# A split moved ahead of the last expert product, filler turns ahead of the first, and result rows asked for by SyncE

## The reference, cut to what matters

```python
def grouped_moe(h, router_w, router_b, w1, w3, w2):        # D = 1024, EXPERT_FF = 256
    s = jax.nn.sigmoid(h @ router_w)                       # 16 scores per token
    ...                                                    # best group, two best experts in it, weights that sum to 1
    y = jnp.zeros_like(h)
    for e in range(N_EXPERTS):
        a = jax.nn.silu(h @ w1[e]) * (h @ w3[e])
        y = y + combine[..., e:e + 1] * (a @ w2[e])
    return y

for i in range(DEPTH):                                     # DEPTH = 2
    ...                                                    # h from norm and modulation, four mixers, gates, w_o: x = x + m[:, 2] * mix
    h2 = modulate(rms_norm(x, norm2_g[i]), m[:, 3], m[:, 4])
    x = x + m[:, 5] * grouped_moe(h2, router_w, router_b, moe_w1[i], moe_w3[i], moe_w2[i])
```

## Time and profile before

| | value |
|---|---|
| median of 3 runs | 2329.77 us (2325.93 to 2334.15) |
| the profiled execution's own time | 2335.57 us |
| its span, first to last instruction | 2333.8 us |
| PE busy | 2124.2 us, 91% of the span |
| DVE busy | 1372.8 us, 59% |
| ACT busy | 991.8 us, 42% |
| mean granted TensorE clock | 0.952 of 2.4 GHz |
| expert stage of layer 0 / layer 1 | about 1043 to 1333 us / 2058 to 2305 us of the span |

### The profile page before, as it was taken

One profiled execution on the slowest core, in us unless ns is written; L12 is line 12 of the kernel. 1 busy time (PEld: TensorE's weight loads), 2 busy tenths in 40 slices (PEclk: granted clock), 3 DMA queues, 4 the chain that ended last, 5 costly groups with the idle time before them and its releaser, 6 DMA issues.

```text
span 2333.8 us, 28756 instructions
## 1 busy us (share of the span) xinstructions
PE 2124.2 (91%) x10673; PEld 1719.5 (74%) x10673; DVE 1372.8 (59%) x1496; ACT 991.8 (42%) x1290; POOL 369.5 (16%) x400
## 2 busy tenths in 40 slices
PE   5879999999989999978999766999999999889994
PEld 3646788888778888877878654668888878778783
DVE  2655455666766433367989666453344454469885
ACT  3645411321211122227878655442422223348882
POOL 3300000000000001003555323000000000025552
PEclk7979999999989999988999887999999999999997
DMA  7020044444655232029999452003334344269993
GB/s 278 1 63 1 19 122 136 140 123 132 190 175 150 73 109 90 28 107 369 388 362 383 169 197 72 1 1 81 100 87 108 95 122 131 73 254 368 368 371 132
DMA packets 247398, 360.00 MB, mean 154 GB/s; under 512 B 22528, under 2 KB 180480, under 8 KB 245760
## 3 DMA queue, kind: packets, MB, share of 16 engines
q1 hardware_dynamic: 219776, 297.65, 39.0%
q0 software_dynamic: 22336, 42.07, 5.2%
q10 hardware_dynamic: 5184, 18.88, 2.1%
HBM read 354.23 MB, written 36.78 MB: 168 GB/s over the span
## 4 chain that ended last, share of the span: by engine, by line
PE 71%; DVE 12%; DMA 8%; ACT 4%; issue 3%; SPq 1%; POOL 0%; ACTq 0%; DVEq 0%; POOLq 0%
PE ps L641 31%; PE ps L629 17%; PE ps L643 7%; DMA RING<-in_moe_w 4%; PE ps L865 4%; DMA MGZ<-in_mod_w 3%; DVE WS L1754 1%; PE ps L1071 1%; PE ps L824 1%; PE ps L849 1%; PE ps L850 1%; PE ps L851 1%; DVE MGZ L1766 1%; PE ps L813 1%; PE ps L1036 1%
## 5 line engine op out<-in xcount | busy, mean ns | idle before, releaser
L641 PE MATMUL ps<-HTH,WS 128*128 128x512 f32 x1664 | 583.1, 398 | 15.4 <-DVE WS L1754 15.3
L641 PEld LDWEIGHTS ps<-HTH,WS 128*128 128x128 f32 x1664 | 313.7, 189 | 92.8 <-DVE WS L1754 18.7
L641 PE MATMUL ps<-HTL,WS 128*128 128x512 f32 x832 | 328.1, 394 | 0.0
L1302 ACT ACTIVATE WS<-RAWB 128x1024 fp32r<-128x1024 f32 (+1 forms) x128 | 162.7, 1272 | 314.9 <-PE ps L643 109.9
L629 PE MATMUL ps<-HTH,MGH 128*128 128x512 f32 x1000 | 281.1, 404 | 12.1 <-DVE MGH L2122 12.1
L1754 DVE TENSOR_TENSOR WS<-RAWB,WS 128x1024 fp32r<-128x1024 f32 (+1 forms) x128 | 190.5, 1489 | 116.5 <-ACT WS L1302 116.4
L629 PE MATMUL ps<-HTL,MGH 128*128 128x512 f32 x800 | 233.0, 404 | 9.4 <-DVE HTL L2132 9.4
L643 PE MATMUL ps<-HTH,WS 128*128 128x256 f32 x832 | 234.6, 282 | 0.0
L629 PEld LDWEIGHTS ps<-HTH,MGH 128*128 128x128 f32 x1000 | 189.4, 194 | 53.6 <-DVE MGH L2122 8.2
L1527 ACT ACTIVATE HTH<-RING 128x2048 fp32r<-128x2048 f32 x100 | 191.2, 1912 | 77.3 <-DMA RING<-in_moe_w 57.9
L641 PE MATMUL ps<-BRH,WS 128*128 128x512 f32 x512 | 182.6, 397 | 3.5 <-DVE BRL L1910 3.5
(11 more groups left out here) (336 smaller groups left out, 3765.1 us busy)
## 6 DMA issues: line engine op xcount, KB each, us to landing
RING<-in_moe_w SPq DMA_DIRECT2D x300, 512.0 KB, 7.7
RAWB<-in_w_in SPq DMA_DIRECT2D x112, 512.0 KB, 4.2
MGZ<-in_mod_w SPq DMA_DIRECT2D x80, 512.0 KB, 4.0
RAWB<-in_w_branch SPq DMA_DIRECT2D x64, 256.0 KB, 4.8
MGZ<-y_rows POOLq DMA_DIRECT2D x20, 512.0 KB, 6.5
RAWB<-in_w_o SPq DMA_DIRECT2D x16, 512.0 KB, 3.9
HTF<-in_mod_w SPq DMA_DIRECT2D x6, 1024.0 KB, 15.0
h_rows<-BR ACTq DMA_DIRECT2D x10, 512.0 KB, 2.6
```

The lines of the kernel that those rows point to most:

```text
L641: last = mm(psb(pair)[:, 0:SEQ], a[:, k0 + k, :], b[:, k, 0:SEQ], start=go, stop=end)
L1302: act_f(parts(s, words(s))[0], raw_slab(r, words(s)), ACT.Copy).then_inc(S("w_hi"), 1)
```

## The change

There are four edits, the same in both layers.

1. The last block's down slab is split already in turn nb - 1, right behind the activation of that block, and not into the down buffers but into the pair of the first up half (`up_hi[0]`, `up_lo[0]`), which no later block needs; the last product reads it from there. In turn nb that split is gone.
2. Block nb is no longer gathered, transposed and split. To drop it, TensorE's and GpSimd's loops end one iteration earlier, and TensorE's last two turns are written out (`expert_turn`).
3. TensorE makes 26 more throwaway transposes behind the transposes of block 0's rows.
4. The rows are read back by SyncE (`expert_rows`) instead of GpSimd. In layer 1's front they stand behind the three `w_in` slabs and ahead of `w_ukv` (tiles 0 to 2), and ahead of the first gate chunk (tiles 3 to 5). GpSimd waits for tile 0's rows and then issues the parameter loads.

```diff
@@ signals
-        **dict.fromkeys(("idx", "xT_ps", "xgT", "xg_lo"), blocks + 1), ...
+        **dict.fromkeys(("idx", "xT_ps", "xgT", "xg_lo"), blocks), ...
@@ SyncE
+            def expert_rows(l, t):
+                p = YPAIR[t]
+                if t == 0:
+                    nb = expert_blocks(W(l))
+                    for j in range(2):
+                        sp.wait_ge(S(f"y_st{j}"), at(f"y_st{j}", l, 16 * ((nb + 1 - j) // 2)))
+                if t >= 3:
+                    sp.wait_ge(S("x_new"), at("x_new", l, t - YPAIR[:t][::-1].index(p)))
+                for k in range(2):
+                    o = k * YROWS + t * P
+                    sp.dma_start(yg[p][k], y_rows[l][o:o + P, :]).then_inc(S(f"yg{p}"), 16)
...
                 for r, pieces in enumerate(loads[l]):
+                    if l and r == len(KVQ_SPLIT):
+                        for t in range(3):
+                            expert_rows(l - 1, t)
+                    if l and r == FIRST:
+                        for t in range(3, tiles(l - 1)):
+                            expert_rows(l - 1, t)
...
+            for t in range(tiles(DEPTH - 1)):
+                expert_rows(DEPTH - 1, t)
             sp.wait_ge(S("x_stored"), 16 * LT)
@@ TensorE
                 gather_T(0, 0)
-                for b in range(3):
+                awake(3, 26)
+                def expert_turn(b):
...
-                    gather_T(b + 1, (b + 1) % 2)
+                    if b + 1 < nb:
+                        gather_T(b + 1, (b + 1) % 2)
                     if b:
                         pe.wait_ge(S("aT_lo"), at("aT_lo", l, b))
+                        if b >= 3:
+                            pe.wait_ge(S("y_sb"), at("y_sb", l, b - 2))
                         pe.wait_ge(S("e_lo"), slab_no(l, 2, b - 1) + 1)
                         down((b - 1) % 2)
...
-                with pe.Fori(0, (nb - 3) // 2) as i:
+                for b in range(3):
+                    expert_turn(b)
+                with pe.Fori(0, (nb - 5) // 2) as i:
...
+                for b in (nb - 2, nb - 1):
+                    expert_turn(b)
                 pe.wait_ge(S("aT_lo"), at("aT_lo", l, nb))
                 pe.wait_ge(S("y_sb"), at("y_sb", l, nb - 2))
                 pe.wait_ge(S("e_lo"), slab_no(l, 2, nb - 1) + 1)
-                down((nb - 1) % 2)
+                down((nb - 1) % 2, (up_hi[0], up_lo[0]))
@@ ScalarE
+                def last_down_split(n):
+                    act.wait_ge(slab_full[n % SLOTS], 16 + 32 * (n // SLOTS + 1))
+                    act.wait_ge(S("h1_ps"), at("h1_ps", l, nb))
+                    act_f(up_hi[0], slot(n % SLOTS), ACT.Copy).then_inc(S("e_hi"), 1)
...
                     if b < nb:
                         silu(b, b % 2, b < 2)
+                    if b + 1 < nb:
                         rows_hi(b + 1)
-                    if b + 1 < nb:
                         up_split(1, slab_no(l, 1, b + 1), b + 1)
+                    if b == nb - 1:
+                        last_down_split(slab_no(l, 2, b))
@@ VectorE
                     if b < nb:
                         hidden(b, b % 2, b < 2)
+                    if b + 1 < nb:
                         rows_lo(b + 1)
-                    if b + 1 < nb:
                         slab_lo(1, slab_no(l, 1, b + 1))
+                    if b == nb - 1:
+                        slab_lo(2, slab_no(l, 2, b), last=True)
@@ GpSimd
-                for t in range(NT):
-                    ...
-                        pool.dma_start(yg[p][k], y_rows[l][o:o + P, :]).then_inc(S(f"yg{p}"), 16)
                 if l + 1 < DEPTH:
+                    pool.wait_ge(S("yg0"), at("yg0", l, 32))
+                    parameters(l + 1)
                     pool.wait_ge(S("x_new"), at("x_new", l, NT))
                     value_ones()
```

More of the change, by code:

```diff
@@ L137, in signals @@
         **dict.fromkeys(("g_prod", "g_ps", "g_sig"), 4 * KD), **dict.fromkeys(("qkT", "qk_hi", "qk_tr"), rounds),
-        **dict.fromkeys(("idx", "xT_ps", "xgT", "xg_lo"), blocks + 1), **dict.fromkeys(("m_hi", "m_lo", "n2_sq", "w_sc", "w_tr", "w_x"), KD),
+        **dict.fromkeys(("idx", "xT_ps", "xgT", "xg_lo"), blocks), **dict.fromkeys(("m_hi", "m_lo", "n2_sq", "w_sc", "w_tr", "w_x"), KD),
         **dict.fromkeys(("up_ps", "up_sb"), 4 * AT), **dict.fromkeys(("br_hi", "br_lo"), 4 * BC),
@@ L143, in signals @@
         "par_g2": 16, "par_p": 16, "par_sb": 32, "x_back": 16 * AT,
-        "xg0": 16 * (blocks // 2 + 1), "xg1": 16 * ((blocks + 1) // 2),
+        "xg0": 16 * ((blocks + 1) // 2), "xg1": 16 * (blocks // 2),
         "y_st0": 16 * ((blocks + 1) // 2), "y_st1": 16 * (blocks // 2), **{f"yg{j}": 32 * YPAIR.count(j) for j in range(3)},
@@ L1080, in hidden, with down @@
                     last.then_inc(S("h_ps" if half else "h1_ps"), 1)
-                def down(j):
-                    w = [a.rearrange("p (k n) -> p k n", k=2) for a in (down_hi, down_lo)]
+                def down(j, w_parts=(down_hi, down_lo)):
+                    w = [a.rearrange("p (k n) -> p k n", k=2) for a in w_parts]
                     for n in range(2):
@@ L1544, in turn_of @@
                         hidden_hi(b - 1)
-                        down_split(slab_no(l, 2, b - 1), b - 1 if b > 1 else None)
+                        if b < nb:
+                            down_split(slab_no(l, 2, b - 1), b - 1 if b > 1 else None)
                     if b >= 2:
@@ L2127, in hidden_lo, with slab_lo @@
                         .then_inc(S("aT_lo"), 1)
-                def slab_lo(kind, n, turn=0):
-                    hi, lo = (down_hi, down_lo) if kind == 2 else (up_hi[kind], up_lo[kind])
+                def slab_lo(kind, n, turn=0, last=False):
+                    hi, lo = (down_hi, down_lo) if kind == 2 and not last else (up_hi[kind % 2], up_lo[kind % 2])
                     dve.wait_ge(S("e_hi"), turn + (n + 1))
@@ L2137, in turn_of @@
                         hidden_lo(b - 1)
-                        slab_lo(2, slab_no(l, 2, b - 1))
+                        if b < nb:
+                            slab_lo(2, slab_no(l, 2, b - 1))
                     if b + 1 < nb:
@@ L2363, in _ @@
                     gather(b + 2, b, b + 2)
-                with pool.Fori(0, (nb - 3) // 2) as i:
+                with pool.Fori(0, (nb - 5) // 2) as i:
                     for j in range(2):
@@ L2368, in _ @@
                         scatter(i * 2 + j, j)
-                for b in range(nb - 3, nb):
+                pool.wait_ge(S("xT_ps"), at("xT_ps", l, nb - 2))
+                gather(nb - 1, 0, nb - 1)
+                for b in range(nb - 5, nb):
                     scatter(b, b % 2)
@@ L2372, in _ @@
                     pool.wait_ge(S(f"y_st{j}"), at(f"y_st{j}", l, 16 * ((nb + 1 - j) // 2)))
-                for t in range(NT):
-                    p = YPAIR[t]
-                    if t == 3 and l + 1 < DEPTH:
-                        parameters(l + 1)
-                    if t >= 3:
-                        pool.wait_ge(S("x_new"), at("x_new", l, t - YPAIR[:t][::-1].index(p)))
-                    for k in range(2):
-                        o = k * YROWS + t * P
-                        pool.dma_start(yg[p][k], y_rows[l][o:o + P, :]).then_inc(S(f"yg{p}"), 16)
                 if l + 1 < DEPTH:
+                    pool.wait_ge(S("yg0"), at("yg0", l, 32))
+                    parameters(l + 1)
                     pool.wait_ge(S("x_new"), at("x_new", l, NT))
```

## The result

The changed kernel took 2316.69 us (median of 6 runs, 2314.71 to 2323.22), the kernel before 2327.61 in the 6 runs beside it. The ratio is 0.9949, 95% interval [0.9931, 0.9967]: faster by 11 us at the medians, where 16.7 were forecast. Over all twelve the mean is 2315.7 us (standard error 1.1), against 2329.2 for the kernel before in all comparisons of this study: 13.5 us. The first six alone would have set me looking for 5 lost us, of which half were the scatter of six runs.

The account below looks back on a forecast made before the run. TensorE was busy for 91% of the span, so only its waits or half-clock stretches could give much. Terms 5.5 + 5.8 + 2.9 + 1.9 + 0.6 = 16.7 us, taken from the median, gave 2313.1 us, range 2305 to 2322.

Parts of the forecast that it names:

- The early split, 5.5 + 5.8: End of each layer's experts: last product starts 3.3 us earlier, and full clock saves 2.2 (layer 0) or 2.5 (layer 1).
- the first rival: Last product of both layers: the clock falls all the same, 4.7 us of the sum gone, 2317.8 us; chance 0.14.
- Rows between the layers, 2.9: Rows read by SyncE between the layers: 2.2 us earlier landing, 0.53 second-tile wait, 0.2 quicker issue; bounds 0.2 to 4.2.
- no row has a pair of such transfers alone: Rows by SyncE: no profile row shows such a pair alone on its queue, so 5.3 us was taken from other transfers.
- The rival that the queue is no matter: Rows by SyncE: data ahead of and beside a pair sets its landing; 0.5 + 0.4 instead of 4.8, 2317 us; chance 0.13.
- the signs that I named against myself: Last product above 4.5 us, pair landing in 7 us or more, or a new wait in layer 1's front.
- Rows at the end, 1.9: Rows read by SyncE at the program's end: 7.0 - 5.3 + 0.2 = 1.9 us; bounds 0.2 to 3.2.
- nothing in the sum grows with the 5.8 us: Whole sum: the profiled execution was 5.8 us above the median, yet its terms were subtracted from the median unchanged.
- Idle turns, 0.3 + 0.3: Ahead of each layer's first product: 26 turns net 0.6 us, half let through, 0.3 per layer, 0.6 in all.
- the less lucky case: Idle turns ahead of the first product: 26 take 4.6 us, so it starts up to 2.0 us late, at full clock.
- The step behind the 0.3: Expert stage: time gained ahead of the stretch waiting for slabs can be lost there, so half of 0.6 is let through.
- Code fetch, the slower side: TensorE's last two written-out turns per layer wait for code; from about 6 us per turn 2337 and above; slower 0.04.

## Why the prediction was right, and where it was not

**The mechanism was right, the sum 3 us too large.** Forecast 16.7; measured 11 over the first six runs and 13.5 over twelve.

**The early split, 5.5 + 5.8: right in its working, a little large on average.** From the last up product to the end of the copy there were 14.1 to 15.1 us in all three profiles of kernels without it. There are 9.0 in 15 and 10.4 to 10.6 in 7 of the 22 ends (eleven profiles, two layers) with it. The part that moves work was there every time and measured 3.6 us instead of 3.3 (the last product begins 4.9 us behind the up product instead of 8.6). The part that came from the clock, 2.2 and 2.5, was there whole in two thirds; in the other third the product took 4.4 to 4.6 us, so that only 1.6 of it was lost. The mean is 5.0 + 5.6. So the first rival, to which I gave 0.14 as if it were true or false for the kernel, is true or false for each execution, and its price of 4.7 us for both ends measured 3.2. Two kernels run on the same chip show it: those with rows behind `w_ukv` and with turns in the front have the same program up to the end of layer 0, and the one has 10.6 there, the other 9.0. Each of the three chips used had both. The Trainium skill, "TensorE: Matmul & The Clock Gate", section What's actually happening, has the lower clock follow idleness of the engine; the trace agrees for the wait of 4.7 us (the product behind it took 4.5 to 5.5 us in all six cases), but here one and the same wait of 2.0 us came out either way.

**Rows between the layers, 2.9: right in size, wrong in cause.** Taken up to the third tile's add, GpSimd's kernels with `w_ukv` ahead needed 23.3 to 23.8 us behind the copy, SyncE's 20.2 to 22.2 in nine profiles: 2.3 us. The step "no row has a pair of such transfers alone" was sound, and 5.3 us per pair was hit (5.2). But I priced the queue where only the order counted: GpSimd with `w_ukv` held back is as fast (21.5 us). That the size came out all the same is luck: the edit changed the order together with the queue. The rival that the queue is no matter is thereby true as to its reason and wrong as to its price, since the change also moves the transfers past each other. Of the signs that I named against myself, one came true: a new wait in layer 1's front, at the third tile, in five of the nine SyncE profiles (the add 9.6 to 10.2 us behind the first instead of 8.2). It costs 1.3 to 1.9 us and is already in the 2.3.

**Rows at the end, 1.9: the mis-sized term.** It measured 0.3. I took 7.0 us from a single execution, and wrote that nothing in the sum grows with the 5.8 us by which that execution was above the median: this row did, by 1.9. The same load took 5.1 to 5.2 in the other four, and SyncE's takes 5.05 to 5.25. What is left is that SyncE issues 0.02 us behind the scatter's landing and GpSimd 0.29. Nothing competes there, so order cannot bring anything either. The Trainium skill, "DMA: Bandwidth & Descriptors", section Specifications, has 0.4 us between the two paths; I set that aside for the row, and as a price for this place it would have been the better one. As a cause it isn't seen: from the issue to the add both paths take the same to 0.2 us.

**Idle turns, 0.3 + 0.3: not resolved by the times.** The product was 2.1 us faster and 2.0 later in layer 0, as worked out for the less lucky case. The runs allow anything from nothing to some 5 us (1.9, standard error 1.8). The other profiles were luckier: from the start of the row transposes to the end of the first product there are 8.3 us on average in the 16 cases with 26 turns and 9.1 in the 10 without, 0.8 us per layer (standard error 0.3). Part of it may be given back at the next block of layer 1, whose up product took 7.3 instead of 5.9 us in four of seven profiles with turns and open waits and in one of five without. The step behind the 0.3, that only half of what is won ahead of the slab-paced stretch comes through, is contradicted by the profile of the run with 86 turns, where all of the delay does; its times do not exclude two thirds.

**Code fetch, the slower side:** the last two written-out turns show no gap (each up product 5.5 us, the product 2.7, in both layers). With 5.0 + 5.6 + 2.3 + 0.3 the measured terms come to 13.2 us without the idle turns, and to 14.8 with 0.8 for them in each layer, beside 13.5 (standard error 1.2) from the times.

## What to carry to other kernels

A term that rests on one row of one execution needs a second look at the same thing, elsewhere in the trace or in a second profile, before it is priced to a tenth. When a transfer moves to another queue, ask first what now stands ahead of it and beside it; the queue itself was worth nothing here, its quicker reaction 0.3 us. Where a slow product follows a wait, split the gain into the work moved, which is certain, and the clock, which is a chance per execution.

## What the runs showed that I had not expected

- The clock at one and the same place is not a property of the kernel. The last product held full clock in 15 and lost it in 7 of 22 cases behind a wait of 2.0 us. The head product in layer 1's front took 2.85 us in ten profiles behind waits of 2.0 to 2.5 us and 5.49 in two behind 2.54 and 2.55, but behind a wait of 1.66 it took 2.85 in one and 4.54 in the other of two kernels whose program is the same there.
- Forty filler transposes in a wait of 5.1 us held the clock in both kernels that had them; without them the row transposes behind it took 1.97 us in all twelve other profiles.
- Delay was not absorbed by a stretch in which the DMA engines are 0.97 busy and which a ring of fixed depth feeds: 13 us more ahead of it cost 9.7 us of time (standard error 2.0) and no less than 13 in the one profile. The ring was full, 16 transfers in, before the first product with and without the delay.
- Open: why the third tile's rows sometimes come 1 to 2 us later (8.2 against 9.6 to 10.2 us behind the first add), in kernels whose code is the same there.
